# A modulation vector's sums moved from VectorE to TensorE, and one column group turned feature-major

## The reference, cut to what matters

```python
mod = silu(c) @ w_ada + b_ada                  # (2048) @ (2048 x 12288)
shift1, scale1, gate1, shift2, scale2, gate2 = split(mod, 6)
h = rmsnorm(x, norm_mix_g) * (1 + scale1) + shift1
proj = h @ w_in                                # (512 x 2048) @ (2048 x 4944)
c_q, c_kv, k_pe, q_m, k_m, v_m, o_m, g_m = split(proj)
```

## Time and profile before

| | |
|---|---|
| median of 3 runs | 2584.14 us (2583.12 to 2587.58) |
| profiled execution, its own time | 2579.41 us |
| its span, first to last instruction | 2577.8 us |
| PE busy | 2352.8 us, 91% of the span |
| DVE busy | 962.4 us, 37% |
| POOL busy | 974.9 us, 38% |
| ACT busy | 716.5 us, 28% |
| bytes moved | 355.16 MB, mean 138 GB/s |

### The profile page before, as it was taken

How to read it: one execution, slowest core, us unless ns; L and a number is a source line. 1 busy time by engine, 2 the same in 40 slices (tenths; PEclk the granted TensorE clock), 3 DMA queues, 4 the chain that set the end, 5 groups by cost and what they waited for, 6 DMA issues and landing times.

```text
span 2577.8 us, 28533 instructions
## 1 busy us (share of the span) xinstructions
PE 2352.8 (91%) x10352; PEld 1932.7 (75%) x10352; DVE 962.4 (37%) x1352; ACT 716.5 (28%) x988; POOL 974.9 (38%) x466
## 2 busy tenths in 40 slices
PE   3669999996788788979999999999999999999998
PEld 3558788875665666867888888888888888888887
DVE  5868666504665537975111102111111012021112
ACT  3223333222334521224212213122122122231221
POOL 2435344431111123434444444444444444444441
PEclk7879999996888888989999999999999999999999
DMA  8767676730103638862233233332332333322322
GB/s 296 243 233 253 195 259 222 272 99 25 37 17 114 234 110 297 301 209 82 99 98 98 96 93 96 98 98 98 98 95 93 97 98 98 98 97 92 95 98 82
DMA packets 176937, 355.16 MB, mean 138 GB/s; under 512 B 13162, under 2 KB 21868, under 8 KB 175472
## 3 DMA queue, kind: packets, MB, share of 16 engines
q1 hardware_dynamic: 168096, 331.34, 39.1%
q10 hardware_dynamic: 8784, 23.07, 2.3%
HBM read 327.09 MB, written 27.28 MB: 137 GB/s over the span
## 4 chain that ended last, share of the span: by engine, by line
PE 74%; DVE 10%; issue 7%; DMA 6%; ACT 1%; POOL 1%; SPq 1%; DVEq 0%; ACTq 0%; POOLq 0%
PE ps L613 24%; PE ps L615 23%; PE ps L614 23%; DVE acc L1402 4%; DMA araw<-in_w_ada 4%; PE ps L647 1%; DVE yc L1553 1%; DVE acc L1399 1%; DMA gb<-g_d 1%; DVE sqacc L1843 0%; DVE pT L1690 0%; DVE pr L1683 0%; DVE stl L1563 0%; DMA wraw<-in_w_in 0%; POOL gbm L588 0%
## 5 line engine op out<-in xcount | busy, mean ns | idle before, releaser
L313 POOL TENSOR_TENSOR wlo<-wraw,whi 128x1024 fp32r<-128x1024 f32 (+3 forms) x384 | 916.0, 2390 | 1151.1 <-ACT whi L308 1150.0
L308 ACT ACTIVATE whi<-wraw 128x1024 fp32r<-128x1024 f32 (+2 forms) x376 | 390.7, 1045 | 1304.7 <-PE ps L615 1173.6
L613 PE MATMUL ps<-h2T,whi 128*128 128x512 f32 x1024 | 399.6, 390 | 3.1 <-DVE h2T L1865 3.1
L614 PE MATMUL ps<-h2T,whi 128*128 128x512 f32 x1024 | 399.3, 390 | 0.0
L615 PE MATMUL ps<-h2T,wlo 128*128 128x512 f32 x1024 | 399.3, 390 | 0.0
L613 PE MATMUL ps<-ah,whi 128*128 128x512 f32 x1024 | 398.3, 389 | 0.0
L614 PE MATMUL ps<-al,whi 128*128 128x512 f32 x1024 | 398.3, 389 | 0.0
L615 PE MATMUL ps<-ah,wlo 128*128 128x512 f32 x1024 | 398.3, 389 | 0.0
L1402 DVE SCALAR_TENSOR_TENSOR acc<-araw,silc,acc 128x512 f32<-128x512 f32 x360 | 352.7, 1040 | 45.6 <-DMA araw<-in_w_ada 45.4
L1879 DVE TENSOR_TENSOR sq<-utmp 128x512 f32<-128x512 f32 x64 | 71.9, 1143 | 609.5 <-ACT utmp L1334 606.2
L1891 DVE SCALAR_TENSOR_TENSOR x1T<-ps,M,x1T 128x512 f32<-128x512 f32 x128 | 87.2, 744 | 558.0 <-PE ps L615 558.0
(11 more groups left out here) (264 smaller groups left out, 2561.7 us busy)
## 6 DMA issues: line engine op xcount, KB each, us to landing
wraw<-in_w_ff SPq DMA_DIRECT2D x256, 512.0 KB, 3.5
araw<-in_w_ada SPq DMA_DIRECT2D x192, 512.0 KB, 5.1
wraw<-in_w_in SPq DMA_DIRECT2D x72, 512.0 KB, 5.6
wraw<-in_w_out SPq DMA_DIRECT2D x32, 512.0 KB, 6.7
xnat<-in_x ACTq DMA_DIRECT2D x4, 1024.0 KB, 7.5
xT_d<-xT ACTq DMA_DIRECT2D x1, 4096.0 KB, 13.4
qk_d<-sth ACTq DMA_DIRECT2D x16, 256.0 KB, 3.1
qk_d<-stl ACTq DMA_DIRECT2D x16, 256.0 KB, 4.7
```

Source lines behind the costliest of these rows:

```text
L308: act.activation(whi[:, slot, 0:kb, 0:cols], wraw[:, slot, 0:kb, 0:cols], ACT.Copy).then_inc(hi_ready, 1)
L313: pool.tensor_tensor(wlo[:, slot, 0:kb, 0:cols], wraw[:, slot, 0:kb, 0:cols], whi[:, slot, 0:kb, 0:cols].bitcast(F), ALU.subtract).then_in ...
L613: pe.matmul(dst, lhs[0], rhs[0], start=start, stop=False)
L614: pe.matmul(dst, lhs[0], rhs[1], start=False, stop=False)
```

## The change

Shift1 and scale1 are summed by TensorE alone. For every unit, 8 fp32 matmuls take a raw 128x128 piece of `w_ada` from `araw` as the stationary operand and one column of `silc` as the moving one, and accumulate over the 16 row tiles into columns 400 and up of bank 7 (`ada_gemv`). A quarter has 16 units, so 128 such matmuls; quarter 0's are placed between the transposes of x, those of quarter q+1 inside quarter q: one call (16 matmuls) before its blocks and one after each row tile but the last. Slots of `araw` are released by a TensorE semaphore, `ada_pe`. `ada_sum` is no longer called in this stage. To free bank 7, group 1 is computed feature-major: 3 feature tiles (128, 128, 80) by 512 tokens in banks 4 to 6, so 9 matmuls of 512 columns in place of 12 of 336 for each row tile; ScalarE copies them to a new tile `kvf` and TensorE transposes them back in 12 pieces during group 2. `kv_quarter` is gone. The x transposes use 7 banks in rotation. The two passes of the loop over groups 3 to 6 are written out.

```diff
@@ helpers
+    def x_bank(t, k):
+        return (4 * t + k) % 7
+    GEMV = 400
@@ sync
+        def first_ada_load(q, u):
+            q0, u0 = (q, u - 4) if u >= 4 else (q - 1, u + 12)
+            if q0 >= 0:
+                sp.wait_ge(ada_pe, 16 * q0 + u0 + 1)
+            k0 = 2 * (u // 2)
+            sp.dma_start(araw[:, u % 4, :, :],
+                         w_ada3[:, k0:k0 + 2, D * (u % 2) + 512 * q:D * (u % 2) + 512 * q + 512]
+                         ).then_inc(ada_loaded[u % 4], 16)
@@ tensor
+        def ada_gemv(q, j):
+            for w in range(2):
+                u = 2 * j + w
+                pe.wait_ge(ada_loaded[u % 4], 16 * (4 * q + u // 4 + 1))
+                for kk in range(2):
+                    kt = 2 * j + kk
+                    for m in range(4):
+                        c = GEMV + 8 * q + 4 * w + m
+                        ins = pe.matmul(ps[:, 7, c:c + 1], araw[:, u % 4, kk, m * P:(m + 1) * P],
+                                        silc[:, kt:kt + 1], start=(kt == 0 and m == 0 and w == 0),
+                                        stop=(kt == KT - 1 and m == 3 and w == 1))
+                ins.then_inc(ada_pe, 1)
+            if j == 7:
+                pe.sem_inc(ada_summed, 1)
...
+            if t == 0:
+                pe.wait_ge(vec_cols, 1)
+                pe.wait_ge(silc_done, 1)
+            ada_gemv(0, 2 * t)
+            ada_gemv(0, 2 * t + 1)
...
         for q in range(4):
-            if q >= 1:
-                pe.wait_ge(ada_read, 2 * q)
-                pe.wait_ge(kv_part, q)
-            ada_sum(q, acc[:, 2 * (q % 2):2 * (q % 2) + 2, :], 7)
-            for n in range(4 * q, 4 * q + 4):
+            pe.wait_ge(ada_read, 2 * (q + 1))
+            if q < 3:
+                ada_gemv(q + 1, 0)
+            def next_gemv(half):
+                if q < 3 and half < 7:
+                    ada_gemv(q + 1, half + 1)
+            for i in range(4):
+                n = 4 * q + i
                 g, b = first_block(n)
-                group_block(n, b, g, hin, GB, True, cols=336 if g == 1 else 512,
+                group_block(n, b, g, hin, GB, g == 0, cols=512 if g == 0 else 336,
                             kready=lambda kt: pe.wait_ge(h_lo, kt + 1), slot=n % RING,
-                            by_quarters=(3,) if g == 1 else ())
+                            beside=lambda k: next_gemv(2 * i + k))
...
+        def kv_transposes():
+            pe.wait_ge(kv_copied, 3)
+            for t in range(TT):
+                for m in range(3):
+                    w = min(P, 336 - m * P)
+                    ins = pe.transpose(ps[:, 4 + t, m * P:m * P + w],
+                                       kvf[0:w, m, t * P:(t + 1) * P], ident[0:w, 0:w])
+                ins.then_inc(kv_T, 1)
...
+                    if b == 2 and isinstance(g, int) and g == 2:
+                        kv_transposes()
@@ vector
-        quarter_units(0, range(6))
...
-            if q >= 1:
-                quarter_units(q, range(4, 7))
-                kv_quarter(q - 1).then_inc(kv_part, 1)
-                quarter_units(q, range(7, 8))
-            ada_cols(q, 7, M_SH1 + 4 * q, M_SC1 + 4 * q)
+            ada_cols(q, 7, M_SH1 + 4 * q, M_SC1 + 4 * q, GEMV + 8 * q)
...
-            modulate(range(4 * q, 4 * q + 4), xT, A1, rstd, utmp, u_done, h_lo,
-                     beside=lambda i: quarter_units(q + 1, [i]) if q < 3 else None)
-        kv_quarter(3).then_inc(bank_free[1], 1)
+            modulate(range(4 * q, 4 * q + 4), xT, A1, rstd, utmp, u_done, h_lo)
```

More of the change, by code:

```diff
@@ L130, in build @@
     low = ExitStack()
+    with ExitStack() as st:
+        kvf = at(st, "kvf", [P, 3, S])
     cqT = [at(low, f"cqT{i}", [P, QL // P, S], R) for i in range(2)]
@@ L225, in build @@
     x_loaded = [sem("x_loaded0"), sem("x_loaded1")]
-    x_T, x_evac, kv_part = sem("x_T"), sem("x_evac"), sem("kv_part")
+    x_T, x_evac = sem("x_T"), sem("x_evac")
+    kv_copied, kv_T = sem("kv_copied"), sem("kv_T")
     def norm_sems(name):
@@ L233, in build @@
     ada_step, ada_summed, ada_read = sem("ada_step"), sem("ada_summed"), sem("ada_read")
+    ada_pe = sem("ada_pe")
     u_done, h_sum, h_hi, h_lo = sem("u_done"), sem("h_sum"), sem("h_hi"), sem("h_lo")
@@ L314, in split_lo, with step_base @@
                            whi[:, slot, 0:kb, 0:cols].bitcast(F), ALU.subtract).then_inc(lo_ready, 1)
+    def step_base(pair):
+        return 32 * pair - 64
     def ada_unit_release(pair, u):
-        return 32 * pair + 4 * (u // 2) + 3 + u % 2
+        return step_base(pair) + 4 * (u // 2) + 3 + u % 2
+    def x_bank(t, k):
+        return (4 * t + k) % 7
+    GEMV = 400
     def norm_sum(pe, sems, bank, squares):
@@ L368, in _, with ada_load @@
         sp.dma_start(wgate[:, :, :], w_in3[:, :, DIN - 16:DIN]).then_inc(gate_loaded, 16)
[L370 to L376, removed]
+        def ada_load(pair, u, col0, col1, raw=araw):
+            if u >= 4:
+                sp.wait_ge(ada_step, ada_unit_release(pair, u - 4))
+            else:
+                sp.wait_ge(ada_step, ada_unit_release(pair - 1, u + 12))
             k0 = 2 * (u // 2)
@@ L380, in ada_load @@
                          ).then_inc(ada_loaded[u % 4], 16)
+        def first_ada_load(q, u):
[6 more added lines that the diff above has]
+                         ).then_inc(ada_loaded[u % 4], 16)
         for q in range(4):
             for u in range(16):
-                ada_load(q, u, 512 * q, D + 512 * q, first=(q == 0 and u < 4))
+                first_ada_load(q, u)
                 if u % 4 == 3:
@@ L394, in later_ada_load @@
             ada_load(pair, u, col0, col0 + 512, raw=raw)
+        sp.wait_ge(ada_pe, 64)
         with sp.Fori(1, 5) as gp:
@@ L620, in group_block @@
         def group_block(n, b, half, act_of, blocks, by_tokens, cols=512, kready=None,
-                        slot=None, by_quarters=()):
+                        slot=None, beside=None):
             slot = b % RING if slot is None else slot
@@ L628, in group_block @@
                     kready(kt)
-                for m in range(4):
+                for m in range(4 if by_tokens else (cols + P - 1) // P):
                     first, last = kt == 0, kt == KB * blocks - 1
-                    if m in by_quarters:
-                        first, last = kt % 4 == 0, kt % 4 == 3
+                    hi = min(cols, (m + 1) * P)
                     if by_tokens:
@@ L637, in group_block @@
                     else:
-                        ins = passes(ps[:, 4 * half + m, :], wtile(slot, k, m * P, (m + 1) * P),
+                        ins = passes(ps[0:hi - m * P, 4 * half + m, :], wtile(slot, k, m * P, hi),
                                      [act_of(i, kt) for i in range(2)], first, last)
-            ins.then_inc(blk_done, 1)
+                if k == KB - 1:
+                    ins.then_inc(blk_done, 1)
+                if beside is not None:
+                    beside(k)
+        def ada_gemv(q, j):
[12 more added lines that the diff above has]
+                pe.sem_inc(ada_summed, 1)
         def ada_sum(pair, tile, bank):
-            pe.wait_ge(ada_step, 32 * (pair + 1))
+            pe.wait_ge(ada_step, step_base(pair + 1))
             for w in range(2):
@@ L729, in in_pair @@
                     group_block(GB * (2 * gp + h) + b, b, h, hin, GB, by_tokens)
-        with pe.Fori(1, 3) as gp:
-            in_pair(gp, False)
+        in_pair(1, False)
+        in_pair(2, False)
         in_pair(3, True)
@@ L1013, in _ @@
             split_hi(act, n, n % RING, n // RING + 1)
-            if b < TT:
+            if b == 0:
                 act.wait_ge(blk_done, 2 * GB)
-                if b < TT - 1:
-                    act.activation(ckv[:, b, :], ps[:, 4 + b, 0:336], ACT.Copy).then_inc(bank_free[1], 1)
+                for m in range(3):
+                    w = min(P, 336 - m * P)
+                    act.activation(kvf[0:w, m, :], ps[0:w, 4 + m, :], ACT.Copy
+                                   ).then_inc(kv_copied, 1)
+            if 1 <= b <= TT:
+                act.wait_ge(kv_T, b)
+                act.activation(ckv[:, b - 1, :], ps[:, 3 + b, 0:336], ACT.Copy).then_inc(bank_free[1], 1)
             if b == 4:
@@ L1379, in _ @@
         dve.wait_ge(silc_done, 1)
+        dve.sem_inc(ada_step, 64)
         def ada_units(pair, us, raw=araw, tile=acc[:, 0:2, :], same=True):
@@ L1400, in ada_units @@
                         else:
-                            dve.wait_ge(ada_step, 32 * pair + i - 1)
+                            dve.wait_ge(ada_step, step_base(pair) + i - 1)
                             dve.scalar_tensor_tensor(dst, src, silc[:, kt:kt + 1], dst, ALU.mult, ALU.add
@@ L1405, in ada_cols @@
         def ada_cols(pair, bank, m0, m1, at=0):
-            dve.wait_ge(ada_summed, pair + 1)
+            if at:
+                dve.wait_ge(ada_pe, 16 * (pair + 1))
+            else:
+                dve.wait_ge(ada_summed, pair + 1)
             for w, m in enumerate((m0, m1)):
```

20 lines of the change are left out of this document (4 added, 16 removed).

## The result

The changed kernel is slower: a median of 2687.15 us (2682.73 to 2700.75, 4 runs) against 2583.63 (2579.08 to 2587.58, 4 runs), 1.0419 times, 95% interval 1.0393 to 1.0444. The prediction said 2694 us, 2615 to 2755.

A forecast was written before the change was run, and what follows sets the result against it. VectorE was taken to pace the opening stage, with TensorE bounding it after the change: group 2 starts 108.7 us later, transposes add 1.4, together 110, a span of 2688; plus 6.3 to the median gives 2694 us, range 2615 to 2755.

The forecast's parts named there:

- What bounds the kernel: Opening stage: VectorE and the slots it releases set the pace; TensorE has some 18 us slack in a 43 us quarter.
- what a matvec costs: One-column fp32 matmul on TensorE: 0.2125 us at the higher clock, 0.4425 at the lower; 128 a quarter.
- End of the first sums: First quarter: first call at the higher clock, seven at the lower, three sets of transposes; sums end at 79.6 us.
- First block: First quarter: 7.4 us from sums to first block matmul, holding the norm broadcast; blocks begin at 87.0 us.
- The middle quarters: Quarters with blocks and matvecs: both clock levels, 69.4 us each, between bounds 46.3 and 92.5; mixed clock, chance 0.62.
- lower throughout: Rival, chance 0.07: dense runs too short to raise the clock in the opening stage; about 2765 us.
- Behind group 2: After the opening stage: 12 transposes add 1.4 us; other small terms together allowed 3 us either way.
- The median: Whole kernel: span 2688 us, plus 6.3 us by which the runs' median lies above the profiled span, 2694 us.
- The clock's mechanism: Opening stage on TensorE: clock rises near a dense run's end, holds through part of the matvecs, then falls again.
- Holds once released: Rival, chance 0.18: matvecs don't raise the clock but keep it from falling; group 2 at 246.1, 2630 us.
- higher throughout: Rival, chance 0.08: higher clock in the whole opening stage, first quarter bound by transfers; group 2 at 210.6, 2594 us.
- Faster: Rival, chance 0.05: long matvec runs overlap their loads, one of two hidden (0.106 us), at the higher clock; 2554 us.

The follow-up runs named there:

- half run: The changed kernel with every second row tile left out of the matrix-vector sums, 64 matvecs a quarter for 128: 2556.92 us, 0.990 of the kernel before.
- swap: The kernel before with two VectorE statements swapped, the next group's first units ahead of the last kv_quarter add: 2569.91 us, 0.9953.
- spread run: The changed kernel with each row tile's 16 matvecs spread between its tiles, 4 to 6 at a time: 2739.54 us, 1.0613 of the kernel before.
- 64-column run: The changed kernel with each matvec's moving operand made 64 equal silc columns, sums whole: 2598.89 us, 1.0077 of the kernel before.
- halves: The changed kernel with scale1 summed by VectorE and shift1 by TensorE, 64 matvecs a quarter: 2575.64 us, 0.9975 of the kernel before.
- last run: The halves kernel with 64-column matvecs, and ScalarE's three first weight splits moved ahead of its norm copy: 2566.6 us, 0.9935 of the kernel before.

## Why the prediction was right, point by point

**What bounds the kernel, and what a matvec costs.** Right. VectorE had set the pace; TensorE took its place at once. Forecast 0.4425 us a matvec at the lower clock, measured 0.4225 in the first quarter; at the lower clock I had divided a duration (3.54 us), at the higher one a distance between starts. The 0.2125 at the higher clock came back in the half run (8 matvecs between 77.57 and 79.27). The Trainium skill's page "TensorE: Matmul & The Clock Gate", section "LDWEIGHTS (loading the stationary operand)", with one duration for both levels, would have given 2628 us; at the lower level the trace has double.

**The terms of the sum**, profiled execution:

| | forecast | measured |
|---|---|---|
| sums of the first quarter end | 79.6 | 79.9 |
| first block | 87.0 | 91.6 |
| from there to the fourth quarter's first block | 203.3 | 221.95 |
| fourth quarter's blocks | 20.5 | 19.5 |
| group 2 starts | 310.8 | 333.1 |
| behind it | +1.4 | -9.6 |
| span against before | +110 | +121.4 |

*End of the first sums.* The 0.3 us are partly luck. The first call, forecast at the higher clock (3.4 us), ran at the lower one (6.8), while the price was 0.02 us too high for the other 112 matvecs (2.2 us) and the three sets of transposes took 10.3 us, not 11.0.

*First block.* I kept 7.4 us from the sums to it and let the first call of quarter 1 fit inside; it took 11.7. The norm broadcast (2.06 us, and a wait of 0.69) stands ahead of that call, which then takes 6.99, so the call ends 9.7 us behind the sums. And with VectorE silent the next engine in line showed: GpSimd has three weight parts (83.63 to 90.2) ahead of the low part of h, and the last 1.96 us, of idle TensorE, are its doing. The forecast named the modulation chain as next and not the splits in its queue.

*The middle quarters* were the mis-sized term: 75.4, 75.1 and 71.5 us from first block to first block, where I had 69.4, 69.4 and 64.5, from the middle of 46.3 and 92.5. The middle was a guess between two bounds and not a reading. Both levels did appear, in group 0's half. In group 1's half the clock stayed at 0.50 but for the end, which I had listed as a ground for "lower throughout" and then left out of the middle.

*Behind group 2.* The allowance of 3 us either way missed the 9.6 us. In the trace of before TensorE waits for 3.7 us for VectorE and 1.2 for GpSimd there and is at 0.50 for 10.2 us, about 5 us lost (an estimate: half of them); none of the three is in the trace after. The wait of VectorE ahead of `kv_quarter(3)`, which the change removes, is the likeliest origin; the swap, which removes it alone, got 4.7 us of this in its trace. The row of 17.59 us idle was in the trace of before and I had not read it.

*The median.* That it came within 7 us is in part luck. Group 2 was 22.3 us later than forecast, and 11 us less than forecast came behind it, which leaves the profiled span 11 us over the forecast's 2688. I then put the median 6.3 us above that span, and it lies 12 below it, because the profiled execution is 11 to 18 us longer than the other three. These have mean clocks of 0.924 to 0.926 against its 0.935, whose record lacks the start; why the profiled one is longer is open.

**The clock's mechanism** was right in outcome: 16 one-column matmuls behind every row tile did not raise it, and in group 0's half it rose near the end of a dense run and fell in or behind the matvecs, as forecast. What I blamed before the spread run, the length of the matvec run, was wrong. The runs show in its place: with 16 one-column matvecs a row tile the clock is lowest where dense runs are shortest (mean 0.50 spread, 0.62 unspread), with half as many it stays up (1.00), and so it does when the moving operand of the same instructions is widened (1.00 with 64 and 128 columns in the later two middle quarters, 0.69 on average with 16).

**The rivals.** "Holds once released" (2630) and "higher throughout" (2594) fell, though in the half run the clock did hold through runs of 8 matvecs. The Trainium skill's page "TensorE: Matmul & The Clock Gate", section "What's actually happening", says activity releases the throttle; TensorE was busy for 75.10 of 75.10 us at 0.61 on average, so being busy was not enough here. The 64-column run, at 2599, shows what the clock of "higher throughout" was worth. That it is only 5 us from 2594 is again two errors: its group 2 starts at 223.5 us, not 210.6, and the gain behind it makes up for most of that. "Lower throughout" (2765) is what the spread run came near to. "Faster" needed loads that overlap; no run showed it.

## What to carry to other kernels

A matrix-vector product on TensorE pays for every weight load and, with one moving column and as many of them as here, for the clock of all that runs beside it; look in the trace for the granted clock in a stretch of such matmuls before moving them in. If they have to be there, repeat the vector into more columns: the instruction costs nearly the same (0.218 us with 64 against 0.2125 with one). It saved 88 us here and still lost: 2599 us against 2569 for the same kernel with the sums on VectorE. When an engine is relieved, read what is queued on the others between the old wait and its reader, and read the idle times of the relieved engine itself: here two statements swapped around a 17.6 us wait of VectorE gave 11 us by the medians. And compare a mixed kernel with each of its parts: the halves were faster than before by what the feature-major part gives alone.

## What the hardware showed that I had not expected

- A matmul of 128 rows by 128 weights in fp32 costs 0.2125 us with 1 moving column, 0.218 with 64 and 0.218 with 128 (3.49 us for 16), from start to start at the higher clock. With 16 such matmuls behind each row tile the width decided whether that clock was granted.
- VectorE's adds with two SBUF operands ran at 0.70 us each alone (1.40 for two) and 2.6 us each beside GpSimd's subtractions (5.15 for two). The Trainium skill, page "SBUF — State Buffer", section "Who interferes with whom", has the two engines contend for a shared port when VectorE has two SBUF inputs and GpSimd reads SBUF; the 5.15 us of the last run agree.
- Executions of some kernels with both clock levels in the opening stage lie far apart: 2648.89 to 2671.28 with the first quarter on VectorE, 2661.95 to 2683.66 with 16 columns, four runs each, against 2573.44 to 2585.9 in 14 runs of the kernel before. The kernel before has both levels too, so the clock as the reason is an assumption.
